# Retention scores in four matrix products instead of six, with the two parts added on VectorE

## The reference

```python
s = jnp.einsum('bnihd,bnjhd->bnhij', qc, kc) * decay_in[None, None]
o_in = jnp.einsum('bnhij,bnjhe->bnihe', s, vc)

def step(state, inp):
    qn, kn, vn = inp
    cross = jnp.einsum('bihd,bhde->bihe', qn, state) * xi[None, :, :, None]
    state = state * chunk_decay[None, :, None, None] + jnp.einsum(
        'bjhd,bjhe->bhde', kn * zeta[None, :, :, None], vn)
    return state, cross
```

## Time and profile before

| | |
|---|---|
| median of 3 executions | 1368.29 us (1368.13 to 1368.42) |
| profiled execution, first to last instruction (span) | 1366.5 us |
| TensorE busy | 1354.6 us, 99% |
| VectorE busy | 1063.1 us, 78% |
| ScalarE busy | 591.4 us, 43% |
| GpSimd busy | 473.3 us, 35% |
| granted TensorE clock, mean | 0.999 of full speed |

### The profile page before, as it was taken

The page is one execution under the profiler, slowest core; times in us unless marked ns, Lnnn a source line. Parts: engine busy times, 40 slices in busy tenths (PEclk is TensorE's granted clock), DMA queues, the critical chain, the costliest instruction groups (busy, mean ns, idle before and its releaser), DMA issues.

```text
span 1366.5 us, 16902 instructions
## 1 busy us (share of the span) xinstructions
PE 1354.6 (99%) x6498; PEld 1138.4 (83%) x6498; DVE 1063.1 (78%) x1053; ACT 591.4 (43%) x801; POOL 473.3 (35%) x349
## 2 busy tenths in 40 slices
PE   9999999999999999999999999999999999999997
PEld 7888888888888888888888888888888888888886
DVE  6898474578877777788888888747776998788887
ACT  7843233323222233234333333438778434433445
POOL 0100232244555554555555666415454001100002
PEclk9999999999999999999999999999999999999999
DMA  9746313322212222355443444657767699945443
GB/s 338 215 128 216 114 56 124 124 77 77 77 50 63 74 62 62 109 154 154 138 140 124 116 146 141 198 193 254 264 229 261 142 327 312 233 164 200 161 86 124
DMA packets 106128, 212.74 MB, mean 156 GB/s; under 512 B 6977, under 2 KB 49089, under 8 KB 101185
## 3 DMA queue, kind: packets, MB, share of 16 engines
q1 hardware_dynamic: 103024, 193.82, 42.4%
q0 software_dynamic: 2880, 17.83, 6.6%
q10 hardware_dynamic: 144, 0.02, 0.0%
HBM read 148.20 MB, written 55.05 MB: 149 GB/s over the span
## 4 chain that ended last, share of the span: by engine, by line
PE 95%; issue 1%; ACT 1%; DVE 1%; POOL 1%; DMA 0%; SPq 0%; POOLq 0%; DVEq 0%; ACTq 0%
PE psum L2488 16%; PE psum L2489 16%; PE psum L2486 16%; PE psum L2623 7%; PE psum L2625 7%; PE psum L2624 7%; PE psum L2413 4%; PE psum L2415 4%; PE psum L2416 4%; PE psum L2430 2%; PE psum L2432 2%; PE psum L2431 2%; PE psum L2531 2%; PE psum L2533 2%; PE psum L2532 2%
## 5 line engine op out<-in xcount | busy, mean ns | idle before, releaser
L2488 PE MATMUL psum<-hc,slots 128*128 128x512 f32 x976 | 379.8, 389 | 0.0
L2486 PE MATMUL psum<-hc,slots 128*128 128x512 f32 x976 | 379.8, 389 | 0.0
L2489 PE MATMUL psum<-hc,slots 128*128 128x512 f32 x976 | 379.8, 389 | 0.0
L1088 ACT ACTIVATE slots<-work 128x1024 fp32r<-128x1024 f32 (+1 forms) x158 | 162.0, 1036 | 435.9 <-PE psum L2489 329.0
L1583 DVE TENSOR_TENSOR slots<-work,slots 128x1024 fp32r<-128x1024 f32 (+1 forms) x158 | 228.6, 1448 | 39.0 <-ACT slots L1088 39.0
L2489 PEld LDWEIGHTS psum<-hc,slots 128*128 128x128 f32 x976 | 183.2, 188 | 38.1
L2486 PEld LDWEIGHTS psum<-hc,slots 128*128 128x128 f32 x976 | 183.2, 188 | 37.5
L2488 PEld LDWEIGHTS psum<-hc,slots 128*128 128x128 f32 x976 | 183.2, 188 | 37.3
L1348 ACT ACTIVATE last_slot<-arena 128x1024 fp32r<-128x1024 f32 x112 | 118.6, 1062 | 163.0 <-PE psum L2625 156.8
L2623 PE MATMUL psum<-last_slot 128*128 128x512 f32 (+1 forms) x452 | 175.3, 388 | 0.0
L2625 PE MATMUL psum<-last_slot 128*128 128x512 f32 (+1 forms) x452 | 175.0, 387 | 0.0
(11 more groups left out here) (214 smaller groups left out, 2331.2 us busy)
## 6 DMA issues: line engine op xcount, KB each, us to landing
work<-w_channel SPq DMA_DIRECT2D x80, 512.0 KB, 3.7
arena<-w_last SPq DMA_DIRECT2D x19, 1024.0 KB, 7.5
qk<-qk_scratch SPq DMA_DIRECT2D x32, 512.0 KB, 3.4
arena<-w_last POOLq DMA_DIRECT2D x9, 1024.0 KB, 11.4
v_raw<-value_scratch SPq DMA_DIRECT2D x32, 256.0 KB, 3.7
arena<-gate_scratch SPq DMA_DIRECT2D x16, 512.0 KB, 7.1
value_c<-w_value SPq DMA_DIRECT2D x10, 512.0 KB, 4.8
rows_of_x<-x_rows SPq DMA_DIRECT2D x8, 512.0 KB, 8.8
```

The lines of the kernel that those rows point to most:

```text
L1088: nc.scalar.activation(slots[:, u % SLOTS, 0, 0:columns_of(u)], src, ACT.Copy).then_inc(w_hi, 1)
L2486: nc.tensor.matmul(bank, slot[:, 0, w], x_high, start=product in STARTS and j == 0, stop=False, skip_group_check=True)
L2488: nc.tensor.matmul(bank, slot[:, 0, w], x_low, start=False, stop=False, skip_group_check=True)
L2489: last = nc.tensor.matmul(bank, slot[:, 1, w], x_high, start=False, stop=j == 3, skip_group_check=True)
```

## The change

In `scores`, k's high part is multiplied by the identity, q's high part and q's low part in one product of 384 columns, where there were one of 256 and one of 128. High x high (with low x high) and high x low so come to lie in two different blocks, 1 and 2, of the PSUM bank, and k turned over in blocks 0 and 3. For this the blocks of q are stored in another order, with an identity block beside each set (five in all, each copied by ScalarE); q and k are loaded by two transfers, and the fourth set of k lies where `unused` and product 2 of the last group were, so that SP waits for that product before `load_step(3)`. On VectorE, `score_decayed` first adds the two blocks (a tensor_reduce over two elements each), waits for that by a semaphore, and then multiplies by the table in SBUF. `o_square` writes its squares into `o_rows`, in float32, and waits until the transposes of two steps before have read it.

```diff
-    qk = sb("qk", HC_AT, [P, 8 * AHEAD + 1, P], F32R)
+    qk = sb("qk", HC_AT, [P, 96, P], F32R)
...
-    unused = sb("unused", HC_AT + 46 * KB, [P, V], BF16)
...
+    score_whole = diag_made
...
+    def q_block(b, low, d):
+        return Q_AT + 5 * b + 1 + 2 * d + low
+    def k_block(b, low, d):
+        return (4 * b if b < AHEAD - 1 else LAST_K_AT) + 2 * d + low
+    def score_bank(s):
+        return psum[:, 4 + s % 2, :].rearrange("p (a c) -> p a c", c=P)
+    def turned_keys(s):
+        return score_bank(s)[:, 0:4:3, :]
...
         def load_step(s):
-            sp.dma_start(qk[:, 8 * (s % AHEAD):8 * (s % AHEAD) + 8, :].bitcast(F32), qk_d[h, n])\
-                .then_inc(qk_in[s % AHEAD], 16)
+            for part, to in enumerate((q_block(b, 0, 0), k_block(b, 0, 0))):
+                sp.dma_start(qk[:, to:to + 4, :].bitcast(F32), qk_d[h, n, :, 4 * part:4 * part + 4]).then_inc(qk_in[b], 16)
...
         for s in range(1, AHEAD):
+            if s == AHEAD - 1:
+                sp.wait_ge(unit_done, unit_at(GROUPS - 1, 2) + 1)
             load_step(s)
...
         def o_square(s):
             act.wait_ge(rows_full, s + 1)
-            nc.scalar.activation(unused[:, :], psum[:, 2 + s % 2, :], ACT.Square, scale=V ** -0.5,
+            if s >= 2:
+                act.wait_ge(o_full, s - 1)
+            nc.scalar.activation(o_rows[:, s % 2, :], psum[:, 2 + s % 2, :], ACT.Square, scale=V ** -0.5,
...
         def identity_beside_q():
-            nc.scalar.activation(qk[:, 8 * AHEAD, :], ident[:, :], ACT.Copy).then_inc(beside_q, 1)
+            for b in range(AHEAD + 1):
+                nc.scalar.activation(qk[:, Q_AT + 5 * b, :], ident[:, :], ACT.Copy).then_inc(beside_q, 1)
...
-            nc.vector.tensor_tensor(scored[:, s % 2, :], psum[:, 4 + s % 2, 0:P], table[:, h, 0:P], ALU.mult)\
+            nc.vector.tensor_reduce(scored[:, s % 2, :], score_bank(s)[:, 1:3, :].rearrange("p a c -> p c a"),
+                                    mybir.AxisListType.X, ALU.add).then_inc(score_whole, 1)
+            dve.wait_ge(score_whole, 8 + s + 1)
+            nc.vector.tensor_tensor(scored[:, s % 2, :], scored[:, s % 2, :], table[:, h, 0:P], ALU.mult)\
                 .then_inc(decayed, 1)
...
             for d in range(2):
+                q, k_high, k_low = q_block(b, 0, d), k_block(b, 0, d), k_block(b, 1, d)
+                if s >= UPDATES:
+                    both, of_q, one, of_q_high = bank[:, 1:3, :], qk[:, q:q + 2, :], bank[:, 1, :], qk[:, q, :]
+                elif d == 0:
+                    both, of_q, one, of_q_high = bank[:, 0:3, :], qk[:, q - 1:q + 2, :], bank[:, 0:2, :], qk[:, q - 1:q + 1, :]
                 else:
+                    both, of_q = bank[:, 1:4, :], qk[:, q:q + 3, :]
+                    one, of_q_high = bank[:, 1:4:2, :], qk[:, q:q + 3:2, :]
-                nc.tensor.matmul(both, qk[:, k_high, :], q_and_identity, start=start, stop=False, skip_group_check=True)
-                nc.tensor.matmul(bank[:, 0, :], qk[:, k_high, :], qk[:, q_low, :], start=False, stop=False,
-                                 skip_group_check=True)
-                last = nc.tensor.matmul(both, qk[:, k_low, :], q_and_identity, start=False, stop=stop,
-                                        skip_group_check=True)
+                nc.tensor.matmul(both, qk[:, k_high, :], of_q, start=d == 0, stop=False, skip_group_check=True)
+                last = nc.tensor.matmul(one, qk[:, k_low, :], of_q_high, start=False, stop=d == 1, skip_group_check=True)
             last.then_inc(score_full, 1)
```

More of the change, by code:

```diff
@@ L170 @@
 AHEAD = 4
+Q_AT, LAST_K_AT = 4 * (AHEAD - 1), 92
 SILU_TILES = (44, 45, 46)
@@ L485, in o_place, with by_halves @@
         return arena[:, at:at + 4, chunk * P:(chunk + 1) * P]
+    def q_block(b, low, d):
[6 more added lines that the diff above has]
+        return score_bank(s)[:, 0:4:3, :]
+    def by_halves(a):
+        return a.rearrange("p (a c) -> p a c", c=P)
     def o_turned(s):
@@ L633, in turn_stores @@
                 store_tp(g, by_chunk(two[m][:, 0, :]), chunks(half, 0))
-                store_tp(g, by_chunk(one[m][:, 0, :]), chunks(half, 2))
-                sp.dma_start(chunks(half, 1), by_chunk(turn_b[n][:, :])).then_inc(turn_out, 16)
+                store_tp(g, by_chunk(one[m][:, 0, :]), chunks(half, 1))
+                sp.dma_start(chunks(half, 2), by_chunk(turn_b[n][:, :])).then_inc(turn_out, 16)
                 sp.dma_start(chunks(half, 3), by_chunk(turn_a[n][:, :])).then_inc(turn_out, 16)
@@ L666, in load_step @@
             n, h = divmod(s, HEADS)
-            sp.dma_start(qk[:, 8 * (s % AHEAD):8 * (s % AHEAD) + 8, :].bitcast(F32), qk_d[h, n])\
-                .then_inc(qk_in[s % AHEAD], 16)
+            b = s % AHEAD
+            for part, to in enumerate((q_block(b, 0, 0), k_block(b, 0, 0))):
+                sp.dma_start(qk[:, to:to + 4, :].bitcast(F32), qk_d[h, n, :, 4 * part:4 * part + 4]).then_inc(qk_in[b], 16)
             sp.dma_start(v_raw[:, s % AHEAD, :], value_d[h, n]).then_inc(v_raw_in[s % AHEAD], 16)
@@ L1248, in score_high @@
                     act.wait_ge(update_full, s - 1)
-                nc.scalar.activation(keys[:, s % 2, 0, :], psum[:, 4 + s % 2, P:P + QK], ACT.Copy,
+                nc.scalar.activation(by_halves(keys[:, s % 2, 0, :]), turned_keys(s), ACT.Copy,
                                      scale=table[:, s % HEADS, P:P + 1]).then_inc(key_hi, 1)
@@ L1862, in key_low @@
             parts = keys[:, s % 2]
-            nc.vector.scalar_tensor_tensor(parts[:, 1, :], psum[:, 4 + s % 2, P:P + QK], table[:, s % HEADS, P:P + 1],
-                                           parts[:, 0, :].bitcast(F32), ALU.mult, ALU.subtract).then_inc(key_ready, 1)
+            nc.vector.scalar_tensor_tensor(by_halves(parts[:, 1, :]), turned_keys(s), table[:, s % HEADS, P:P + 1],
+                                           by_halves(parts[:, 0, :]).bitcast(F32), ALU.mult, ALU.subtract)\
+                .then_inc(key_ready, 1)
         def score_low(s):
@@ L2506, in scores @@
         def scores(s):
-            b, bank = s % AHEAD, psum[:, 4 + s % 2, :].rearrange("p (a c) -> p a c", c=P)
-            pe.wait_ge(qk_in[b], 16 * (s // AHEAD + 1))
+            b, bank = s % AHEAD, score_bank(s)
+            pe.wait_ge(qk_in[b], 32 * (s // AHEAD + 1))
             if s >= 2:
@@ L2549, in rows @@
                     c = slice(d * V, (d + 1) * V)
-                    last = product_of(bank, (qk[:, 8 * b + d, :], qk[:, 8 * b + 2 + d, :]),
+                    last = product_of(bank, (qk[:, q_block(b, 0, d), :], qk[:, q_block(b, 1, d), :]),
                                       [state_parts[:, h, part, c] for part in range(2)], False, d == 1)
@@ L2578, in retention_begins @@
             if product == 7:
-                pe.wait_ge(beside_q, 1)
+                pe.wait_ge(beside_q, AHEAD + 1)
                 pe.wait_ge(sum_made, 5 * (GROUPS - 1))
```

6 lines of the change are left out of this document (removed).

## The result

The changed kernel takes 1383.49 us (median of four runs, 1383.04 to 1383.63) where the kernel before takes 1368.36 (1368.13 to 1368.65, beside it on the chip): a ratio of 1.0109, 95% interval 1.0097 to 1.0122. It is 15.1 us slower; the forecast was 13.7 slower.

A forecast was written before the change was run, and what follows sets the result against it. The prediction took a closed VectorE-ScalarE-VectorE ring of waits, 4.61 us a step against TensorE's 4.5, to bound the retention steps. Its terms, 9.0 + 2.9 + 0.5 + 1.3 = 13.7 us, gave 1382.0 us, range 1375.5 to 1387.5.

The forecast's parts named there:

- the middle: The 20 periods from step 7 to step 27, 92.11 us before; forecast to grow by 9.0 and 2.9 us.
- The ring: Steps 7 to 26, closed VectorE-ScalarE-VectorE chain between new_states: the added reduce lengthens each period by 0.45, 9.0 us in all.
- The held multiplication: Steps 7 to 26: in ten steps GpSimd's L976 delays the multiplication, now reading two SBUF tiles, by 0.29; 2.9 us.
- Before step 7: First steps: saving 0.5 in the first four scores, reduce costs in steps 3 to 6; +0.5 us, between -0.8 and +2.5.
- After step 27: Last steps: two more scores on the way to rows(30), 0.9, and o_square(30) waiting for transposes, 0.44; 1.3 us.
- The block of score products: TensorE, each of 28 steps: four products take 0.57 us where six took 0.69, saving 0.12.
- The update's wait: TensorE's first product of update would wait in nearly every step, by 0.8 us on average.
- What costs nothing: Four identity copies, second q/k load, SP's new wait, keys from other blocks, o_square's wait except in the last two steps: free.
- that TensorE leads: Rival: TensorE bounds the kernel, VectorE's 22% idle time takes the reduce, 4.3 us are gained; 1364.0 us, chance 5%.
- The multiplication not held: Rival: GpSimd does not hold the multiplication, or is held instead; 1379.1 us, 1375.0 with a cheap reduce; chance 22%.
- The slow reduce: Rival: the strided reduce on VectorE takes 0.72 us, up to 18.8 us slower, 1387.1 us; chance 20%.

The follow-up runs named there:

- reduce_to_psum: Kernel before plus VectorE's reduce and multiplication only, six products kept, the reduce writing to PSUM and the multiplication reading it there: 1379.80 us.
- products_alone: Changed kernel without the tensor_reduce: VectorE multiplies the first score part straight from PSUM, q low times k high left out; 1368.55 us.
- the new order: From step 7 on, both halves of the state's split come ahead of the next keys and score: changed kernel 1368.09 us, kernel before 1367.26.
- reduce_alone: Kernel before with only VectorE's reduce, semaphore wait and multiplication from SBUF added, six score products kept: 1383.38 us.
- state_first_after: Changed kernel with the state's split ahead of the next step's keys and score from step 7 on: 1368.09 us.
- state_first_before: Kernel before with the state's split ahead of the next step's keys and score from step 7 on, nothing else changed: 1367.26 us.

## Why the prediction was right

The mechanism was the forecast's, and its size came within 1.4 us. The closeness is partly luck: the middle was forecast 0.3 too long, from a ring term that was too small and a hold that was too large, and one term outside it was a third of what it should be. By its own terms:

- *The ring, 20 x 0.45 = 9.0.* Right, a little too small. The reduce takes 0.419 and the pair starts 0.45 apart; reduce_to_psum shows this term alone as 9.45, and products_alone and the new order show that it is a cost of the ring and not of VectorE's load.
- *The held multiplication, 10 x 0.29 = 2.9.* Right in place and count, a little too large: held ones take 0.53 to 0.54 instead of 0.29, 10 x 0.24 = 2.4. GpSimd's instruction ends 2.04 after `new_state` starts (958.27 - 956.23) instead of 2.06, the multiplication 0.14 behind it instead of 0.15, and a free one takes 0.29 instead of 0.28: 0.04 in all. Taking the hold away gave 2.35 back.
- *Before step 7, +0.5.* Too small: 1.47. This is the term that makes most of the difference. The forecast thought of the reduce in steps 3 to 6 and took 0.5 because TensorE was to be covered there by waits for GpSimd. There were none: in the kernel before, TensorE stands idle once between its first score product and step 7, for 0.50 us, and what it waits for is `score_low`. Without the products the pair costs 2.06 there (reduce_alone, 48.01 against 45.95); with one operand in PSUM 0.62 (reduce_to_psum); so the reduce makes 0.62, the two SBUF operands 1.44, and the products give 0.59 back, each good to some 0.3. VectorE's multiplications of this stretch in the changed kernel:

```profile
926.65 0.95 DVE L1885 TENSOR_TENSOR scored<-scored,table 128x128 f32<-128x128 f32 x1
...
931.43 1.39 DVE L1885 TENSOR_TENSOR scored<-scored,table 128x128 f32<-128x128 f32 x1
```

GpSimd's, which hold them (926.16 + 1.30 = 927.46, and 931.38 + 1.29 = 932.67; they end 0.14 and 0.15 later):

```profile
926.16 1.30 POOL L998 TENSOR_TENSOR v_parts<-v_raw,v_parts 128x512 fp32r<-128x512 f32 x1 [0.65 <-ACT v_parts L1262]
...
931.38 1.29 POOL L998 TENSOR_TENSOR v_parts<-v_raw,v_parts 128x512 fp32r<-128x512 f32 x1 [1.60 <-ACT v_parts L1262]
```

and TensorE, which is the one that waits:

```profile
929.39 0.50 PE L2558 MATMUL psum<-v_parts,score 128*128 128x512 f32 x1 [0.90 <-DVE score L1898]
...
934.60 0.50 PE L2558 MATMUL psum<-v_parts,score 128*128 128x512 f32 x1 [0.48 <-DVE score L1898]
```

In the kernel before, the first of these waits was 0.50 (at 929.27) and the second wasn't there: 0.40 + 0.48 = 0.88 of the 1.47. Taken from the first score product to successive starts of `new_state`, the loss is 0.99 at 934.47 (933.27 in the kernel before), 1.20 at 939.00 (937.59) and 1.47 at 946.10 (944.42). The offset of L976 was worked out for the middle only; that it holds for the ring and not ahead of it was missed. The hold itself isn't new in these two steps. In the kernel before it lay on `state_low`, which also has two SBUF operands and takes 1.22 when free:

```profile
926.50 2.12 DVE L1885 TENSOR_TENSOR state_parts<-state,state_parts 128x1024 fp32r<-128x1024 f32 x1
...
931.07 1.69 DVE L1885 TENSOR_TENSOR state_parts<-state,state_parts 128x1024 fp32r<-128x1024 f32 x1
```

Now the multiplication has the hold, and `state_low` behind it takes 1.21 both times. From the start of `score_decayed` to the end of `state_low` it is 2.54 instead of 2.32 in the first step and 2.96 instead of 1.89 in the second. So the second step costs most, and there GpSimd also starts later: 0.39 after the reduce starts, where it was 0.49 ahead of the multiplication.

- *After step 27, 0.9 + 0.44 = 1.3.* Right in both parts: reduce_alone, which has the two scores without the wait of `o_square`, is 0.99 longer at the end, and the wait adds 0.48 (16.97 to 17.45), 0.50 when taken away. Together 1.47.
- *TensorE.* The block of score products went from 0.69 to 0.58, where 0.57 was said. By the table that the prediction quotes from the Trainium skill (TensorE: Matmul & The Clock Gate, Back-to-back issue gap) the four were an estimated 0.54 and the saving 0.01; the trace has 0.58 and 0.11. (The same section gives that table for a product on its own and says that it is too low for small products in a stream with weight loads, which the prediction left out; the trace agrees as to the direction, 0.115 against an estimated 0.056 for 128 columns.) *The update's wait, 0.8 on average*: the weight load's is 14.1 / 16 = 0.88; 103.72 / 20 = 5.19 a period less TensorE's shortest steps in state_first_after, 4.42, is 0.77.
- *What costs nothing.* The four more identity copies are hidden. ScalarE in the changed kernel:

```profile
895.30 1.10 ACT L1413 ACTIVATE qk<-ident 128x128 fp32r<-128x128 f32 x5
...
898.88 1.06 ACT L1110 ACTIVATE slots<-work 128x1024 fp32r<-128x1024 f32 x1 [2.47 <-PE psum L2518]
```

They end at 896.40 and ScalarE is then idle for 2.47 us, where it was 3.27. The split loads, SP's wait and the reading of the keys from blocks 0 and 3 show nothing either: products_alone has them all, and its time is that of the kernel before.

The rivals: that TensorE leads is refuted in this order (products_alone), and true in the other one for the six products (state_first_before). The multiplication not held would have been 1379.1; the kernel in which it isn't held took 1379.80. The slow reduce is refuted by its 0.42. The five differences in the table add up to the 14.9 between the two profiled spans.

## What to carry to other kernels

When two engines are nearly level, the busy shares don't say which one leads: find the closed ring of waits, and price an edit by whether its instruction is on it. Here the same edit cost 11.6 us in one order and gained 1.1 in another, so look at the order first and at the instructions after it. When an operand moves from PSUM to SBUF, check what GpSimd does at that moment in every stage, not in one: the hold on the multiplication was 0.24 us in the middle and up to 1.1 in the start, where part of it had lain on another instruction before. And take a stage's length at a landmark of the engine that you ask about: 20 steps gained 1.12 us at VectorE's `new_state`, and 17 of them 1.67 at TensorE's score products.

## What was not expected

- A tensor_reduce of 128 x 256 f32 from PSUM, reading pairs 512 bytes apart, takes 0.419 us, about as long as a tensor_tensor of 256 elements from PSUM (0.411); pairs of the same element (reduce_alone) take 0.42 as well.
- A VectorE instruction of 0.29 took 1.39 us when it started 0.05 after GpSimd's: the hold went on for as long as GpSimd's instruction ran. In the kernel before, the hold was GpSimd's when VectorE had started first.
- The product behind one of 384 columns follows at 0.18 us, between 0.11 behind one of 256 and 0.23 behind one of 512.
- The profile of products_alone is 0.9 us shorter than that of the kernel before while its median is the same. Its first score product starts 1.1 us earlier, ahead of everything that was changed. Differences of less than 1 us can be read from single profiles only between landmarks.
